# One of four weight sums per seven-product step: an adding transfer within SBUF in place of GpSimd

## The chip, the core and the metric

The kernel runs on one core of one Trainium2 chip, in one launch. Its time is device time in microseconds. The kernel before was timed three times: 1987.64, 1987.86 and 1988.36 us, with a median of 1987.86.

Five engines work from instruction queues of their own and meet only at semaphores: TensorE (PE in the profile; PEld is its weight load), VectorE (DVE), ScalarE (ACT), GpSimd (POOL) and SyncE (SP), which only issues transfers here.

## What is computed

The reference is one inference step of a two-layer encoder for 640 tokens (512 of a prompt, 8 streams of 16). Each layer is

```python
x = x + 0.5 * swiglu(rms_norm(x, norm_g[layer, 0]), w_gate, w_up, w_down)   # 1024 -> 2816 -> 1024
x = x + mixer(rms_norm(x, norm_g[layer, 1]))                                # attention and convolution, or pooling
x = x + 0.5 * swiglu(rms_norm(x, norm_g[layer, 2]), w_gate, w_up, w_down)

def swiglu(h, w_gate, w_up, w_down):
    return (jax.nn.silu(h @ w_gate) * (h @ w_up)) @ w_down
```

all in float32. The four feed-forward blocks (passes one to four in this text, `ffn0` to `ffn3` in the kernel) hold nearly all the work, and the change lies in them alone.

## The kernel before

**Products.** A float32 value is kept as a high part in TensorE's float32r form and a low part, the rest. Each product is three matmuls: high by high, high by low, low by high. ScalarE makes the high part by a copy that rounds (`fast_high`), DVE the low part by a subtraction (`fast_low`).

**Seven products for eight.** The hidden width of 2816 is 22 chunks of 128, in groups of 4, 6, 6 and 6 (`GROUPS`). Group 0 is done plainly. For the other three a step takes a 2 by 2 block of weights and a 2 by 2 block of inputs and forms seven block products instead of eight, in the manner of Strassen and Winograd; this needs sums of weight blocks. A pass has 26 such steps (`STEPS`, numbered 0 to 25): an *input step* handles one hidden chunk (gate and up: 7 products of 4 x 3 matmuls, weights 128x512 per block), an *output step* two output chunks of the down matrix (7 products of 3 x 3 matmuls, blocks of 128x384). Steps 0 to 5, 10 to 15 and 20 to 25 are input steps, 6 to 9 and 16 to 19 output steps.

**The weight sums.** The landed weights of a step are four blocks, `raw[0]` to `raw[3]`. GpSimd makes four sums in `block_and_weight_sums`, each as two instructions of half the columns (`weight_sum`, line 2401):

```python
weight_sum(raw[2], raw[2], raw[3], ALU.add, width)               # the block sum, in place
weight_sum(sums[:, 0], raw[2], raw[0], ALU.subtract, width)      # first sum
weight_sum(sums[:, 1], raw[3], sums[:, 0], ALU.subtract, width)  # second sum
weight_sum(sums[:, 2], raw[1], sums[:, 0], ALU.subtract, width)  # last sum
```

The first sum waits for part 3 of the step before to be split, because `sums` has one buffer; the last sum waits for part 4.

**Splits.** A step's weights go to TensorE in four parts: part 1 is `raw[0:2]`, part 2 is `raw[2:4]` after the block sum, part 3 the first and second sum, part 4 the last sum. In the time of step s ScalarE splits parts 3 and 4 of step s, then parts 1 and 2 of step s+1 (`in_step`), with the copies and activations that read finished products between; DVE follows the same order with the low parts.

**Loads.** SP loads the weights of step s+2 into the buffer of step s (two buffers, `in_raw`). The up half waits for part 2 of step s and for its second sum, the gate half also for its last sum (`in_free`). In each pass, after step 21's loads, SP waits for a product of step 19 and puts two loads of the down matrix (`out_raw`) in the queue ahead of step 22's weights.

**TensorE's order.** In step s TensorE runs the products of slots 0, 4, 1, 2, 6 of step s with those of slots 3 and 5 of step s-1 between (`product_order`). Slots 0 and 1 read part 1, slots 4 and 5 part 2, slots 2 and 3 part 3, slot 6 part 4. The first product of step s writes a bank that is free once DVE has made the low hidden product of step s-2 (`hidden_low`).

Of the kernel before, what the change touches and what calls it, by code (L numbers as in the profile page):

```python
# [9 lines left out]
ALU = mybir.AluOpType  # L10
# [71 lines left out]
N_STEPS = len(STEPS)  # L82
# [42 lines left out]
def product_at(s, slot):  # L125

    return len(PRODUCT_AT) * (s // N_STEPS) + PRODUCT_AT[s % N_STEPS, slot]
# [60 lines left out]
def landed(n):  # L188

    return 32 * (n // 2 + 1) + (32 if n >= IN_CHUNK["mix"] + 1 else 0)  # L190
# [17 lines left out]
def wait(eng, sem, value):  # L208

    if not isinstance(value, int) or value > 0:  # L210
        eng.wait_ge(sem, value)
# [35 lines left out]
def build(nc, ins, outs):  # L247
# [7 lines left out]
    with ExitStack() as stack:  # L255
# [131 lines left out]
        def sem(name):  # L387
            return keep(nc.semaphore(name))


        in_landed = [sem(f"in_landed{i}") for i in range(2)]
# [40 lines left out]

        sum_done, fast_hi, fast_split = sem("sum_done"), sem("fast_hi"), sem("fast_split")
        prod_mm, evac_done, gate_done = sem("prod_mm"), sem("evac_done"), sem("gate_done")
        block_made, block_hi, block_lo = sem("block_made"), sem("block_hi"), sem("block_lo")
# [74 lines left out]
        def in_free(eng, n, tile=0):  # L512

            old = n - 2
            if old < 0:
                return
            phase = [name for name, first in IN_CHUNK.items() if first <= old][-1]
            f = old - IN_CHUNK[phase]
            if phase in FFN_INDEX and f >= PLAIN:
                s = N_STEPS * FFN_INDEX[phase] + f - PLAIN  # L520
                eng.wait_ge(fast_split, 4 * s + 2)
                eng.wait_ge(sum_done, 4 * s + 4 - tile)
            else:
                eng.wait_ge(in_split, 2 * (SPLIT_CHUNK[phase] + f) + 2)

# [2 lines left out]
        def split_source(s, part):  # L528

            if part in (3, 4):  # L530
                return sums[:, 0:2, 0:width_of(s)] if part == 3 else sums[:, 2:3, 0:width_of(s)]
            return step_raw(s, load_number(s))[part - 1]

        def split_target(tensor, s, part):

            slots = tensor[:].rearrange("p j t (h k) c -> p (j t h) (k c)", h=2)
            chosen = {1: slice(0, 2), 2: slice(4, 8, 3) if s % N_STEPS % 2 else slice(4, 6), 3: slice(2, 4), 4: slice(6, 7)}[part]
            return slots[:, chosen, 0:width_of(s)]

        def step_raw(s, n):  # L540

            width = width_of(s)
            return [in_raw[:, n % 2, t, 0:2 * width // P].rearrange("p (h k) c -> p h (k c)", h=2) for t in range(2)]

        def width_of(s):

            return 4 * P if STEPS[s % N_STEPS][0] == "in" else 3 * P

        def load_number(s):

            return IN_CHUNK[FFN_PHASE[s // N_STEPS]] + PLAIN + s % N_STEPS
# [46 lines left out]
        def _(sp):  # L598
            def load_ffn_in(phase, layer, which, f):
                n = IN_CHUNK[phase] + f  # L600
                in_free(sp, n)
                for t, w in enumerate((w_gate, w_up)):
                    sp.dma_start(in_raw[:, n % 2, t],
                                 w[layer, which].rearrange("(k p) c -> p k c", p=P)[:, :, f * P:f * P + P]).then_inc(in_landed[n % 2], 16)
# [9 lines left out]
            def load_mix_in(c):  # L614
                n = IN_CHUNK["mix"] + c
                slot = n % 2
                in_free(sp, n)
                kind, j = MIX_CHUNKS[c]
                if kind == "q":

                    for g in range(2):
                        for t in range(2):
                            at = g * 256 + (2 * j + t) * 64
                            sp.dma_start(in_raw[:, slot, t, :, g * 64:g * 64 + 64], wi[:, :, at:at + 64]).then_inc(in_landed[slot], 16)
                    return
                at = {"kv": (512, 640), "conv": (1280 + 128 * j, 1792 + 128 * j), "gate": (768 + 256 * j, 896 + 256 * j)}[kind]
                for t in range(2):
                    sp.dma_start(in_raw[:, slot, t], wi[:, :, at[t]:at[t] + P]).then_inc(in_landed[slot], 16)
# [11 lines left out]
            def load_pool():  # L640
                n = IN_CHUNK["pool"]
                in_free(sp, n)
                for t in range(2):
                    src = pool_w[0, 2 * t:2 * t + 2].rearrange("g (k p) c -> p (g k) c", p=P)
                    dst = in_raw[:, n % 2, t].rearrange("p (q m) c -> p q (m c)", m=2)
                    sp.dma_start(dst, src).then_inc(in_landed[n % 2], 16)
# [584 lines left out]
        def _(act):  # L1231
# [63 lines left out]
            def fast_high(s, part):  # L1295


                n = load_number(s)
                act.wait_ge(in_landed[n % 2], landed(n))
                if s % N_STEPS:  # L1300
                    act.wait_ge(prod_mm, max(product_at(s - 1, slot) for slot in {1: (0, 1), 2: (4,), 3: (2, 3), 4: (6,)}[part]))
                if part == 2 and s % N_STEPS > 1:
                    act.wait_ge(prod_mm, product_at(s - 2, 5))
                if part > 1:
                    act.wait_ge(sum_done, 4 * s + {2: 1, 3: 3, 4: 4}[part])
                act.activation(split_target(in_hi, s, part), split_source(s, part), ACT.Copy).then_inc(fast_hi, 1)  # L1306

            def block_split(name):
                hi, _, made = block_parts[name]
                act.activation(hi[:], made[:], ACT.Copy).then_inc(block_hi, 1)  # L1310
# [331 lines left out]
            for step, (c, half) in enumerate(MIX_UNITS):  # L1642
# [21 lines left out]
                if step == 2:  # L1664
                    act.wait_ge(kv_turned, 1)
                    first, second = (psum[:, bank].rearrange("p (a b) -> p a b", a=4) for bank in (6, 7))
# [715 lines left out]
        def _(pool):  # L2382
            def less(index, made, a, b, newest):

                pool.wait_ge(block_made, 8 * index + MADE[newest])
                for k in range(4):
                    last = pool.tensor_tensor(made[:, k], a[:, k], b[:, k], ALU.subtract)
                last.then_inc(block_made, 1)
# [9 lines left out]
            def weight_sum(to, a, b, op, width):  # L2398

                for part in (slice(0, width // 2), slice(width // 2, width)):  # L2400
                    last = pool.tensor_tensor(to[:, part], a[:, part], b[:, part], op)  # L2401
                last.then_inc(sum_done, 1)

            def block_and_weight_sums(phase, index):

                if index == 3:
                    pool.wait_ge(rows_stored, 16 * 9)
                less(index, mix_f[1], b22_f, b12_f, "B22")
                less(index, b12_f, b12_f, b11_f, "T3")
                less(index, mix_f[0], b22_f, b12_f, "T1")  # L2410
                less(index, mix_f[2], b21_f, mix_f[0], "T2")
                for i in range(N_STEPS):
                    s = N_STEPS * index + i
                    n, width = load_number(s), width_of(s)
                    own = step_raw(s, n)
                    raw = [own[t][:, h] for t in range(2) for h in range(2)]
                    pool.wait_ge(in_landed[n % 2], landed(n))
                    weight_sum(raw[2], raw[2], raw[3], ALU.add, width)
                    if i == 0:
                        pool.wait_ge(block_lo, 7 * index + BLOCKS.index("B21") + 1)  # L2420
                    if s:
                        pool.wait_ge(fast_split, 4 * (s - 1) + 3)
                    pool.wait_ge(sum_done, 4 * s + 1)
                    weight_sum(sums[:, 0], raw[2], raw[0], ALU.subtract, width)
                    pool.wait_ge(sum_done, 4 * s + 2)
                    weight_sum(sums[:, 1], raw[3], sums[:, 0], ALU.subtract, width)
                    if s:
                        pool.wait_ge(fast_split, 4 * (s - 1) + 4)
                    weight_sum(sums[:, 2], raw[1], sums[:, 0], ALU.subtract, width)
# [19 lines left out]
            pool.wait_ge(line_stored, 16)  # L2449

            block_and_weight_sums("ffn0", 0)
            squares_sum(NORM["mix"], LAST_HALVES)
            pool.wait_ge(out_mm, OUT_UNIT["mix"])
# [20 lines left out]


            block_and_weight_sums("ffn1", 1)
            squares_sum(NORM["ffn2"], LAST_HALVES)
            block_and_weight_sums("ffn2", 2)
            pool.wait_ge(out_mm, OUT_UNIT["ffn2"] + 17)
            pool.wait_ge(conv_stored, 16 * 2)  # L2480
# [36 lines left out]
```

## Time and profile before

| | |
|---|---|
| median of three runs | 1987.86 us |
| the profiled execution | 1988.24 us |
| its span, first to last instruction | 1986.4 us |
| TensorE busy (matmuls) | 1978.6 us, 13462 matmuls |
| DVE / ACT / POOL busy | 1418.2 / 932.5 / 964.0 us |
| granted TensorE clock, mean | 0.999 of full speed |
| moved by DMA | 165.28 MB, mean 83 GB/s |

A timeline row merges neighbouring instructions of one line and form: start, length, engine, line, operation, output and inputs, shape, number of instructions; a bracket at its end is the idle time before it and what ended that. A matmul row is longer than the distance to the next, since matmuls are pipelined: the distance between starts is the pace.

### The profile page before, as it was taken

How to read it: one execution, taken by the hardware profiler on the slowest of the kernel's cores; microseconds unless marked ns; L12 is line 12 of the kernel's file. 1: busy time of each engine (PE TensorE's matmuls, PEld its weight loads, DVE VectorE, ACT ScalarE, POOL GpSimd, SP SyncE). 2: the span in 40 equal slices, each digit the busy share in tenths (PEclk: the TensorE clock that was granted, in tenths of full speed). 3: DMA queues.
4: the chain of work that ended last, by engine and by line, in shares of the span. 5: the costliest groups of instructions: out<-in, count | busy, mean ns of one | idle time of the engine just before them, and what ended most of it. 6: DMA issues, size and time to landing. Idle time of an engine off the chain costs nothing. (4 is left out here: it accounts for less than half of the span.)

```text
span 1986.4 us, 35197 instructions
## 1 busy us (share of the span) xinstructions
PE 1978.6 (100%) x13462; PEld 1957.5 (99%) x13462; DVE 1418.2 (71%) x2263; ACT 932.5 (47%) x1642; POOL 964.0 (49%) x1043
## 2 busy tenths in 40 slices
PE   9999999999999999999999999999999999999998
PEld 8999999999999999999999999999999999999998
DVE  5778687664766667878766668778767866878665
ACT  6354454543434435445455345454545535455443
POOL 2556666632000055676663336666743355666643
PEclk9999999999999999999999999999999999999999
DMA  6232324323222223232432222323332223232412
GB/s 162 74 86 70 101 70 117 101 58 95 66 64 65 56 73 86 77 95 69 117 102 75 64 65 75 96 80 91 102 109 70 67 57 86 77 99 65 122 38 86
DMA packets 312853, 165.28 MB, mean 83 GB/s; under 512 B 15539, under 2 KB 310271, under 8 KB 312688
## 3 DMA queue, kind: packets, MB, share of 16 engines
q1 hardware_dynamic: 307840, 157.31, 28.4%
q0 software_dynamic: 2672, 4.65, 1.0%
q8 instruction: 109, 1.79, 0.4%
q10 hardware_dynamic: 2176, 1.07, 0.2%
q14 instruction: 56, 0.46, 0.1%
HBM read 159.01 MB, written 4.00 MB: 82 GB/s over the span
## 5 line engine op out<-in xcount | busy, mean ns | idle before, releaser
L2401 POOL TENSOR_TENSOR sums<-in_raw,sums 128x256 f32<-128x256 f32 (+1 forms) x416 | 440.1, 1088 | 12.1 <-DVE in_lo L1751 3.9
L2401 POOL TENSOR_TENSOR sums<-in_raw 128x256 f32<-128x256 f32 (+1 forms) x208 | 179.9, 885 | 429.7 <-DVE in_lo L1751 377.4
L895 PE MATMUL psum<-xg_hi,in_lo 128*128 128x320 f32 x1152 | 356.0, 309 | 0.0
L893 PE MATMUL psum<-xg_hi,in_hi 128*128 128x320 f32 x1152 | 355.9, 309 | 0.0
L894 PE MATMUL psum<-xg_lo,in_hi 128*128 128x320 f32 x1152 | 355.9, 309 | 0.0
L1751 DVE TENSOR_TENSOR in_lo<-in_raw,in_hi 128x1024 fp32r<-128x1024 f32 (+1 forms) x208 | 271.9, 1309 | 42.5 <-ACT in_hi L1306 42.2
L893 PE MATMUL psum<-mix_hi,in_hi 128*128 128x320 f32 x864 | 267.0, 309 | 0.0
L894 PE MATMUL psum<-mix_lo,in_hi 128*128 128x320 f32 x864 | 267.0, 309 | 0.0
L895 PE MATMUL psum<-mix_hi,in_lo 128*128 128x320 f32 x864 | 267.0, 309 | 0.0
L1306 ACT ACTIVATE in_hi<-in_raw 128x1024 fp32r<-128x1024 f32 (+1 forms) x208 | 205.0, 991 | 111.7 <-PE psum L895 111.7
L744 PE MATMUL psum<-xg_hi,in_hi 128*128 128x320 f32 x800 | 252.3, 315 | 0.9 <-DVE in_lo L1792 0.6
L746 PE MATMUL psum<-xg_hi,in_lo 128*128 128x320 f32 x800 | 247.2, 309 | 0.0
L745 PE MATMUL psum<-xg_lo,in_hi 128*128 128x320 f32 x800 | 247.1, 309 | 0.0
L1306 ACT ACTIVATE in_hi<-sums 128x1024 fp32r<-128x1024 f32 (+1 forms) x208 | 156.6, 790 | 159.7 <-PE psum L895 124.2
L894 PEld LDWEIGHTS psum<-xg_lo,in_hi 128*128 128x128 f32 x1152 | 216.2, 188 | 0.0
L895 PEld LDWEIGHTS psum<-xg_hi,in_lo 128*128 128x128 f32 x1152 | 216.2, 188 | 0.0
L893 PEld LDWEIGHTS psum<-xg_hi,in_hi 128*128 128x128 f32 x1152 | 216.2, 188 | 0.0
L1751 DVE TENSOR_TENSOR in_lo<-sums,in_hi 128x1024 fp32r<-128x1024 f32 (+1 forms) x208 | 196.2, 967 | 18.1 <-ACT in_hi L1306 15.6
L744 PE MATMUL psum<-f_hi,f_out_hi 128*128 128x320 f32 x640 | 198.7, 311 | 0.3
L745 PE MATMUL psum<-f_lo,f_out_hi 128*128 128x320 f32 x640 | 197.8, 309 | 0.0
L746 PE MATMUL psum<-f_hi,f_out_lo 128*128 128x320 f32 x640 | 197.7, 309 | 0.0
L2401 POOL TENSOR_TENSOR in_raw<-in_raw 128x256 f32<-128x256 f32 (+1 forms) x208 | 168.9, 832 | 20.5 <-DMA in_raw<-in_ffn_w_gate 20.5
(267 smaller groups left out, 4560.9 us busy)
## 6 DMA issues: line engine op xcount, KB each, us to landing
in_raw<-in_ffn_w_gate SPq DMA_DIRECT2D x87, 512.0 KB, 5.2
in_raw<-in_ffn_w_up SPq DMA_DIRECT2D x86, 512.0 KB, 4.0
in_raw<-in_ffn_w_down SPq DMA_DIRECT2D x64, 384.0 KB, 4.0
out_raw<-in_ffn_w_down SPq DMA_DIRECT2D x32, 384.0 KB, 3.5
out_raw<-in_ffn_w_down SPq DMA_DIRECT2D x32, 256.0 KB, 2.9
in_raw<-in_mix_w_in SPq DMA_DIRECT2D x14, 512.0 KB, 4.6
out<-y_nat SPq DMA_DIRECT2D x5, 512.0 KB, 3.1
in_raw<-in_mix_w_in SPq DMA_DIRECT2D x8, 256.0 KB, 4.5
```

Source lines behind the costliest of these rows:

```text
L744: pe.matmul(dst, w_hi, v_hi, start=first, stop=False)
L745: pe.matmul(dst, w_hi, v_lo, start=False, stop=False)
L746: return pe.matmul(dst, w_lo, v_hi, start=False, stop=last)
L893: pe.matmul(dst, w_hi[:, k], v_hi, start=k == 0 and slot in (0, 1, 4), stop=False, skip_group_check=True)
L894: pe.matmul(dst, w_hi[:, k], v_lo, start=False, stop=False, skip_group_check=True)
L895: end = pe.matmul(dst, w_lo[:, k], v_hi, start=False, stop=k == wide - 1, skip_group_check=True)
L1306: act.activation(split_target(in_hi, s, part), split_source(s, part), ACT.Copy).then_inc(fast_hi, 1)
L1751: dve.tensor_tensor(split_target(in_lo, s, part), split_source(s, part), split_target(in_hi, s, part).bitcast(F32), ALU.subtract).then_inc ...
L2401: last = pool.tensor_tensor(to[:, part], a[:, part], b[:, part], op)
```

## The change

The block sum leaves GpSimd's arithmetic. In its place GpSimd issues a transfer whose source is `raw[3]` and whose destination is `raw[2]`, with the addition done by the transfer (`accum_op=ALU.add`). It reports on a semaphore of its own, `blocks_added`, which the first sum on GpSimd and part 2 on ScalarE now wait for. `sum_done` counts three sums per step instead of four. The transfer for step s+1 is issued between the second and the last sum of step s; the block sum for step s+1 stood behind the last sum of step s.

```diff
--- before.py
+++ after.py
@@ -432,6 +432,7 @@
 
 
 
+        blocks_added = sem("blocks_added")
         sum_done, fast_hi, fast_split = sem("sum_done"), sem("fast_hi"), sem("fast_split")
         prod_mm, evac_done, gate_done = sem("prod_mm"), sem("evac_done"), sem("gate_done")
         block_made, block_hi, block_lo = sem("block_made"), sem("block_hi"), sem("block_lo")
@@ -519,7 +520,7 @@
             if phase in FFN_INDEX and f >= PLAIN:
                 s = N_STEPS * FFN_INDEX[phase] + f - PLAIN
                 eng.wait_ge(fast_split, 4 * s + 2)
-                eng.wait_ge(sum_done, 4 * s + 4 - tile)
+                eng.wait_ge(sum_done, 3 * s + 3 - tile)
             else:
                 eng.wait_ge(in_split, 2 * (SPLIT_CHUNK[phase] + f) + 2)
 
@@ -1301,8 +1302,10 @@
                     act.wait_ge(prod_mm, max(product_at(s - 1, slot) for slot in {1: (0, 1), 2: (4,), 3: (2, 3), 4: (6,)}[part]))
                 if part == 2 and s % N_STEPS > 1:
                     act.wait_ge(prod_mm, product_at(s - 2, 5))
-                if part > 1:
-                    act.wait_ge(sum_done, 4 * s + {2: 1, 3: 3, 4: 4}[part])
+                if part == 2:
+                    act.wait_ge(blocks_added, 16 * (s + 1))
+                elif part > 2:
+                    act.wait_ge(sum_done, 3 * s + part - 1)
                 act.activation(split_target(in_hi, s, part), split_source(s, part), ACT.Copy).then_inc(fast_hi, 1)
 
             def block_split(name):
@@ -2401,6 +2404,13 @@
                     last = pool.tensor_tensor(to[:, part], a[:, part], b[:, part], op)
                 last.then_inc(sum_done, 1)
 
+            def add_in_place(s):
+
+                n = load_number(s)
+                second = step_raw(s, n)[1]
+                pool.wait_ge(in_landed[n % 2], landed(n))
+                pool.dma_start(second[:, 0], second[:, 1], accum_op=ALU.add).then_inc(blocks_added, 16)
+
             def block_and_weight_sums(phase, index):
 
                 if index == 3:
@@ -2409,21 +2419,23 @@
                 less(index, b12_f, b12_f, b11_f, "T3")
                 less(index, mix_f[0], b22_f, b12_f, "T1")
                 less(index, mix_f[2], b21_f, mix_f[0], "T2")
+                add_in_place(N_STEPS * index)
                 for i in range(N_STEPS):
                     s = N_STEPS * index + i
                     n, width = load_number(s), width_of(s)
                     own = step_raw(s, n)
                     raw = [own[t][:, h] for t in range(2) for h in range(2)]
-                    pool.wait_ge(in_landed[n % 2], landed(n))
-                    weight_sum(raw[2], raw[2], raw[3], ALU.add, width)
                     if i == 0:
                         pool.wait_ge(block_lo, 7 * index + BLOCKS.index("B21") + 1)
                     if s:
                         pool.wait_ge(fast_split, 4 * (s - 1) + 3)
-                    pool.wait_ge(sum_done, 4 * s + 1)
+                    pool.wait_ge(blocks_added, 16 * (s + 1))
+                    wait(pool, sum_done, 3 * s)
                     weight_sum(sums[:, 0], raw[2], raw[0], ALU.subtract, width)
-                    pool.wait_ge(sum_done, 4 * s + 2)
+                    pool.wait_ge(sum_done, 3 * s + 1)
                     weight_sum(sums[:, 1], raw[3], sums[:, 0], ALU.subtract, width)
+                    if i + 1 < N_STEPS:
+                        add_in_place(s + 1)
                     if s:
                         pool.wait_ge(fast_split, 4 * (s - 1) + 4)
                     weight_sum(sums[:, 2], raw[1], sums[:, 0], ALU.subtract, width)
```

On GpSimd, second pass, steps 21 and 22, the kernel before has these rows: the block sum of step 21 (its second half), its three sums, then the block sum of step 22 (the row that waits for `in_landed1`, the landed weights) and the first sum of step 22.

```order
L2401 TENSOR_TENSOR in_raw<-in_raw 128x256
L2401 TENSOR_TENSOR sums<-in_raw 128x256 [waits sum_done,fast_split]
L2401 TENSOR_TENSOR sums<-in_raw 128x256
L2401 TENSOR_TENSOR sums<-in_raw,sums 128x256 [waits sum_done]
L2401 TENSOR_TENSOR sums<-in_raw,sums 128x256
L2401 TENSOR_TENSOR sums<-in_raw,sums 128x256 [waits fast_split]
L2401 TENSOR_TENSOR sums<-in_raw,sums 128x256
L2401 TENSOR_TENSOR in_raw<-in_raw 128x256 [waits in_landed1]
L2401 TENSOR_TENSOR in_raw<-in_raw 128x256
L2401 TENSOR_TENSOR sums<-in_raw 128x256 [waits sum_done,fast_split]
```

The same place in the changed kernel, from the first sum of step 21 to the second sum of step 22:

```order
L2404 TENSOR_TENSOR sums<-in_raw 128x256 [waits sum_done,blocks_added,fast_split]
L2404 TENSOR_TENSOR sums<-in_raw 128x256
L2404 TENSOR_TENSOR sums<-in_raw,sums 128x256 [waits sum_done]
L2404 TENSOR_TENSOR sums<-in_raw,sums 128x256
L2412 DMA in_raw<-in_raw 128x512 [waits in_landed1]
L2404 TENSOR_TENSOR sums<-in_raw,sums 128x256 [waits fast_split]
L2404 TENSOR_TENSOR sums<-in_raw,sums 128x256
L2404 TENSOR_TENSOR sums<-in_raw 128x256 [waits sum_done,blocks_added,fast_split]
L2404 TENSOR_TENSOR sums<-in_raw 128x256
L2404 TENSOR_TENSOR sums<-in_raw,sums 128x256 [waits sum_done]
```

The wait for `in_landed1` has moved from behind the last sum of step 21 (the row that waits for `fast_split` alone) to ahead of it, and the row that carries it is an issue of a transfer.

On ScalarE, at the same step of the second pass, the kernel before has parts 3 and 4 of step 21, the split of a hidden block (`f_hi`), the copy of a product (`t`), part 1 of step 22, the activation of the low gate, part 2 of step 22:

```order
L1306 ACTIVATE in_hi<-sums 128x1024 [waits sum_done,prod_mm,in_landed0]
L1306 ACTIVATE in_hi<-sums 128x512 [waits sum_done,prod_mm,in_landed0]
L1379 ACTIVATE f_hi<-t2a 128x320 [waits hidden_done]
L1375 ACTIVATE t_51<-psum 128x320 [waits evac_done,prod_mm]
L1306 ACTIVATE in_hi<-in_raw 128x1024 [waits prod_mm,in_landed1]
L1364 ACTIVATE gate_low_74<-gate_low_74 128x320 [waits evac_done]
L1306 ACTIVATE in_hi<-in_raw 128x1024 [waits prod_mm,sum_done,in_landed1]
```

and the changed kernel:

```order
L1309 ACTIVATE in_hi<-sums 128x1024 [waits sum_done,prod_mm,in_landed0]
L1309 ACTIVATE in_hi<-sums 128x512 [waits sum_done,prod_mm,in_landed0]
L1382 ACTIVATE f_hi<-t2a 128x320 [waits hidden_done]
L1378 ACTIVATE t_51<-psum 128x320 [waits evac_done,prod_mm]
L1309 ACTIVATE in_hi<-in_raw 128x1024 [waits prod_mm,in_landed1]
L1367 ACTIVATE gate_low_74<-gate_low_74 128x320 [waits evac_done]
L1309 ACTIVATE in_hi<-in_raw 128x1024 [waits prod_mm,blocks_added,in_landed1]
```

Nothing moves on ScalarE; part 2 (the last row) waits for `blocks_added` where it waited for `sum_done`.

## Rows read from the trace of the kernel before

**Rows 1.** Busy time of each engine (us, x instructions), TensorE clock, DMA, by stretches.
```profile
705.00:995.00 290.00, 290.00 (x1976) 289.56 (x1975) 217.34 (x325) 136.06 (x223) 181.72 (x196) 1.00 0.30 82
...
1918.00:1986.00 68.00, 63.23 (x441) 62.46 (x439) 33.93 (x60) 22.67 (x42) 16.57 (x16) 0.99 0.18 63
```

**Rows 2.** Who TensorE waited for: us, times, longest; first and last of five.
```profile
PE psum L1026 <- DVE mean_r L2142: 1.1, 1, 1.1
...
PE psum L744 <- DVE x L1830: 0.2, 1, 0.2
```

**Rows 3.** TensorE timeline, 992 to 995: start, us, engine, line, operation.
```profile
992.71 0.31 PE L893 MATMUL psum<-xg_hi,in_hi 128*128 128x320 f32 x1
...
994.47 0.31 PE L893 MATMUL psum<-xg_hi,in_hi 128*128 128x320 f32 x1
```

**Rows 4.** GpSimd by groups: busy us, mean ns, idle before.
```profile
L2401 POOL TENSOR_TENSOR in_raw<-in_raw 128x256 f32<-128x256 f32 x144 | 118.1, 840 | 20.5 <-DMA in_raw<-in_ffn_w_gate 20.5
...
L2401 POOL TENSOR_TENSOR in_raw<-in_raw 128x192 f32<-128x192 f32 x64 | 50.9, 815 | 0.0
...
L2456 POOL DMA_DIRECT2D ck_nat<-in_cache_attn_k x1 | 1.0, 952 | 0.0
...
L2468 POOL DMA_DIRECT2D out<-kv_rows x1 | 0.6, 550 | 0.0
```

**Rows 5.** GpSimd timeline, 955 to 1005, second pass.
```profile
958.52 3.72 POOL L2401 TENSOR_TENSOR sums<-in_raw,sums 128x192 f32<-128x192 f32 x4
...
966.27 1.69 POOL L2401 TENSOR_TENSOR sums<-in_raw 128x256 f32<-128x256 f32 x2 [2.63 <-DVE in_lo L1751]
968.05 4.81 POOL L2401 TENSOR_TENSOR sums<-in_raw,sums 128x256 f32<-128x256 f32 x4
972.81 1.44 POOL L2401 TENSOR_TENSOR in_raw<-in_raw 128x256 f32<-128x256 f32 x2
...
978.34 4.81 POOL L2401 TENSOR_TENSOR sums<-in_raw,sums 128x256 f32<-128x256 f32 x4
988.59 1.80 POOL L2401 TENSOR_TENSOR in_raw<-in_raw 128x256 f32<-128x256 f32 x2 [5.44 <-DMA in_raw<-in_ffn_w_gate]
```

**Rows 6.** DMA issues, KB each, median us to landing; then all of `in_raw`.
```profile
cv_nat<-in_cache_attn_v POOLq DMA_DIRECT2D x1, 512.0 KB, 5.7
...
out<-kv_rows POOLq DMA_DIRECT2D x4, 64.0 KB, 2.2
...
DMA to landing us min/median/max: 3.1/4.4/9.6
```

**Rows 7.** ScalarE timeline, 955 to 1005.
```profile
974.04 1.58 ACT L1306 ACTIVATE in_hi<-sums 128x1024 fp32r<-128x1024 f32 x2 [0.93 <-PE psum L895]
...
985.92 1.58 ACT L1306 ACTIVATE in_hi<-sums 128x1024 fp32r<-128x1024 f32 x2 [1.37 <-PE psum L895]
...
987.76 0.42 ACT L1375 ACTIVATE t<-psum 128x320 f32<-128x320 f32 x1
989.45 1.07 ACT L1306 ACTIVATE in_hi<-in_raw 128x1024 fp32r<-128x1024 f32 x1 [1.27 <-PE psum L895]
```

**Rows 8.** Who GpSimd waited for: us, times, longest.
```profile
POOL in_raw L2401 <- DMA in_raw<-in_ffn_w_gate: 20.5, 4, 5.4
```

**Rows 9.** GpSimd timeline, 335 to 355, first pass.
```profile
343.29 2.00 POOL L2401 TENSOR_TENSOR in_raw<-in_raw 128x256 f32<-128x256 f32 x2 [4.86 <-DMA in_raw<-in_ffn_w_gate]
```

**Rows 10.** DVE timeline, 955 to 1005.
```profile
988.75 1.03 DVE L1921 TENSOR_TENSOR f_lo<-t2a,f_hi 128x320 fp32r<-128x320 f32 x1
...
990.54 1.81 DVE L1751 TENSOR_TENSOR in_lo<-in_raw,in_hi 128x1024 fp32r<-128x1024 f32 x1 [0.36 <-ACT in_hi L1306]
992.28 0.49 DVE L1896 TENSOR_TENSOR psum<-psum,gate_low 128x320 f32<-128x320 f32 x1
992.68 1.36 DVE L1751 TENSOR_TENSOR in_lo<-in_raw,in_hi 128x1024 fp32r<-128x1024 f32 x1
993.96 0.48 DVE L1921 TENSOR_TENSOR f_lo<-psum,f_hi 128x320 fp32r<-128x320 f32 x1
```

## The prediction

> **What bounds the kernel now.** I read four views in this order: the busy time of each engine by stretches, TensorE's list of waits, GpSimd's list of waits, and the timelines of single engines around one step. The first answers nearly the whole question. In the middle stretch of the second feed-forward pass TensorE is busy 290.00 us of 290.00; in the last 68 us of the program it is busy 63.23 [rows 1]. Its waits come to five entries, of which the longest is 1.1 us and the shortest 0.2 us, and none stands on the seven-product lines 893 to 895 [rows 2]. TensorE starts a matmul every (994.47 - 992.71) / 12 = 0.147 us without a hole [rows 3], and at that pace an input step (84 matmuls) lasts 12.3 us and an output step (63) 9.2 us. So the time is TensorE's work, and nothing that GpSimd does today is waited for where the change acts. The change can win almost nothing; the question is only whether it makes TensorE wait.
>
> **What goes.** The change takes 208 GpSimd instructions away: 144 of 840 ns and 64 of 815 ns, 118.1 + 50.9 = 169 us of GpSimd time [rows 4]. Worth on the path: nothing, since GpSimd idles in every step. The gain is bounded by what TensorE idles in these stretches, 0.00 us.
>
> Beside DVE instructions that read two operands from SBUF the same GpSimd sum takes far longer: a pair runs 1.44 us at one place and, as half of 4.81, 2.4 us at another [rows 5]. The Trainium skill's page "SBUF — State Buffer" (SBUF: two separate sides) says that a GpSimd operation that reads SBUF and such a DVE operation exclude each other for the whole instruction; by it the change also shortens DVE's low parts, and if DVE were waited for, up to those 169 us would count. The trace agrees on the lengthening, but TensorE's waits for DVE come to 1.1 us at most and none lies on the seven-product lines [rows 2]. That rule's gain is rival 3 below.
>
> **What comes.** 104 accumulating transfers issued by GpSimd. Issuing costs GpSimd 0.55 us for 128 rows (the `kv_rows` store), and 0.95 us for a transfer of many short pieces (`ck_nat`) [rows 4]. This one has 128 rows of 2 or 1.5 KB, like `kv_rows`; I take 0.55 and keep 0.95 as the far end. How long it takes to land no row shows, since no transfer before adds. The nearest rows are the GpSimd-issued transfers of 64 KB at 2.2 us and of 512 KB at 5.7 us; the longest landing of any load into `in_raw` is 9.6 us [rows 6]. Here 256 KB (192 KB in output steps) are read, added to what is read at the destination, and written; I take 4 us, nearer the middle of 2.2 and 5.7, and keep 2.2 and 9.6 as ends.
>
> The Trainium skill's page "Collectives: The Full Stack" (The bandwidth ceiling) says that an adding transfer pays for two source reads, not for the addition. By that it moves like 512 KB, an estimate of 5.7 us from the same row instead of 4; no run here shows it yet. The next paragraph shows that the sum is the same with either.
>
> **What covers it.** The transfer for step s+1 is issued when GpSimd has finished the second sum of step s, and what it makes is wanted when GpSimd takes up the first sum of step s+1. Around the end of the output steps the second sum of step 19 ends at 958.52 + 3.72 / 2 = 960.4 and the first of step 20 starts at 966.27: 5.9 us [rows 5]. So 4 us, 5.7 us too, cost nothing: the GpSimd idle time (waiting for DVE) hides them. Past that there is more cover: the two sums of step 20 end at 968.05 + 2.4 = 970.5, and ScalarE takes them up at 974.04 [rows 5, 7], 3.5 us later. A single landing of 9.4 us would do no harm. ScalarE's split of the added block itself comes later than GpSimd's first sum. The second new cost, 0.55 us on GpSimd ahead of the last sum of every step, falls into the same idle time, and so does the 0.55 us by which the next gate load (which waits for the last sum) leaves later.
>
> **The one place without cover.** The transfer's wait for the landed weights now stands ahead of the last sum of the step before; until now it stood behind it. Four times in the program, 20.5 us in all, GpSimd waits there [rows 8]: at step 22 of each pass, whose weights are queued behind two loads of the down matrix. In the second pass the wait lasts 5.44 us and ends at 988.59; in the first 4.86, that is 0.6 us less late against TensorE's pace [rows 5, 9]; passes three and four repeat the two values (the four make the 20.5). Before, the last sum of step 21 had been done since 978.34 + 4.81 = 983.15. Now it is queued behind this wait, and behind it ScalarE's fourth part of step 21, DVE's, and everything that follows them in their order:
> - GpSimd: wait ends 988.6, issue 0.55, last sum 1.44 (a pair with DVE idle, as DVE then is): 990.6.
> - ScalarE: fourth part 0.6 (the pair of 1.58 less 1.07 for a part of the third's size, a little rounded up), to 991.2; then the hidden split and the copy, 0.7 from the end of that pair to the end of the copy [rows 7]: 991.9. TensorE's last product of step 21 needs this copy and DVE's fourth low part (about 991.9) and starts at 992.71 [rows 3]: it still holds, by 0.8 us. Then the first part of step 22, 1.07: 993.0.
> - DVE: low fourth part until 991.9; then hidden low and gate, 990.54 - 988.75 less the 0.36 of idle time = 1.43 [rows 10]: 993.3; low first part of step 22, 1.74 to the next start: 995.05; the hidden product, 0.49: 995.5.
> - TensorE's first product of step 22 needs both of these and starts at 994.47 today [rows 3]. It is late by 1.05 us.
>
> If DVE runs alone (its hidden low 0.48 rather than 1.03, its low part 1.36 rather than 1.81 [rows 10]), 1.0 us goes and nothing is late. So passes two and four lose 0 to 1.1 us each, passes one and three 0 to 0.5: together 0 to 3.2 us, and I take the middle, 1.6. With the far ends (issue 0.95, the last sum contended at 2.4) each pass loses 1.4 more: 8.8 us. A lost microsecond of TensorE isn't made up later, as it has no idle time to give back.
>
> **The sum.** The profiled execution took 1988.24 us, a span of 1986.4 and 1.84 around it, and lies 0.38 above the median of the three runs, 1987.86. 1988.24 - 0 + 1.6 = 1989.8 in its terms, 1989.5 against the median. Less than 0.2% (4 us) is no change that a measurement of this kernel can tell.
>
> **Rivals.**
> 1. The wait at step 22 weighs more: slower. Mechanism as above, with the far ends of the two prices: 8.8 us, 1996.7; it counts as slower once the four passes lose more than 4 us, that is one microsecond each. For it: every link stands in order behind the landed weights. Against it: DVE is idle when that sum runs, and the issue resembles the 0.55 us row. Chance 0.18.
> 2. The adding transfer is slow everywhere: slower. At 9.6 us the loop of an output step (two sums, 3.7 us, and the transfer) takes 13.3 us against TensorE's 9.2, 4.1 us lost per step. The first landing of four is late by 9.6 - 5.9 - 3.5 = 0.2 us, the fourth by 0.2 + 3 x 4.1 = 12.5; there are eight such groups of four: 100 us, 2088. It begins to decide at 9.2 - 3.7 = 5.5 us kept up over several steps. For it: no row shows an addition, and the loads share the transfer engines. Against it: 5.7 us is the landing of twice the bytes. Chance 0.06.
> 3. Faster, as GpSimd and DVE are relieved. This needs TensorE idle time, of which the passes have none. Even all 68.00 - 63.23 = 4.77 us of its idle time in the last stretch [rows 1], which the change doesn't touch, would only just reach 0.2%: 1983.1. Chance 0.02.
>
> My forecast, no change within 0.2% with 0 to 3.2 us lost, has 0.74. The slower cases make 0.18 + 0.06, and 0.24 is what I give to slower by over 0.2%; faster 0.02. The range goes from 1987.0 (nothing lost, and the spread of the runs below the median) to 1996.0, which takes in nearly all of rival 1 and leaves out rival 2 and the far end.
>
> **What will show it.** Right: GpSimd loses its sums on `in_raw` (about 170 us busy less), gains 104 issues of about 0.55 us, and the adding transfers land within 2.2 to 5.9 us; GpSimd's wait for the gate weights at step 22 is now ahead of the last sum of step 21, four times; TensorE's waits on the seven-product lines come to at most about 3 us, all at the first product of step 22. Wrong: landing above 6 us, GpSimd or ScalarE waiting for the added block in most steps, or TensorE idle in the output steps; or a wait at step 22 well above 1 us a pass.

## The result, and the profile after

The changed kernel takes 2020.03 us (median of four runs, 2019.15 to 2021.21) against 1988.11 of the kernel before (four runs, 1987.64 to 1988.83): a ratio of 1.016, 95% interval 1.0147 to 1.0173. It is 32 us slower, where 1989.5 was forecast in a range that ended at 1996.0. The profiled span grew from 1986.4 to 2017.5 us, 31.1 more.

Read in the order of the forecast, the first view already tells that the passes have holes: the same stretch as in [rows 1], and the last 68 us of the program.

```profile
705.00:995.00 290.00, 284.33 (x1932) 283.00 (x1931) 217.99 (x320) 131.70 (x215) 145.01 (x168) 1.00 0.40 95
...
1949.00:2017.00 68.00, 63.31 (x442) 62.54 (x440) 33.93 (x60) 22.68 (x42) 16.57 (x16) 0.99 0.18 63
```

TensorE is busy 284.33 of 290 us, where it was busy for all of them; the end of the program is as it was. Who TensorE waited for (us in all, times, longest), beside [rows 2]:

```profile
PE psum L894 <- DVE pair_low L1899: 20.8, 16, 1.3
PE psum L894 <- DVE psum L1899: 1.9, 3, 0.9
PE psum L894 <- DVE x L1942: 1.9, 2, 1.0
PE psum L745 <- DVE f_out_lo L1749: 1.9, 4, 0.5
```

Five new entries, all for DVE, none for GpSimd or for a transfer; the fifth, of 0.2 us, is left out here. The first is the finding: 16 waits for `pair_low`, the low hidden product of the odd input steps, four in each pass (at steps 3, 5, 13 and 15). The next views show one of them, at step 3 of the second pass. TensorE first, beside [rows 3]:

```profile
792.16 0.31 PE L896 MATMUL psum<-xg_hi,in_lo 128*128 128x320 f32 x1
793.76 0.41 PE L894 MATMUL psum<-xg_hi,in_hi 128*128 128x320 f32 x1 [1.29 <-DVE pair_low L1899]
```

From start to start that is 1.60 us in place of 0.147. Counted this way the 16 holes cost 23.4 us, four at the start of the first output stage 2.5, three at step 22 of passes two to four 2.4, and two on the fold of `x` 2.2: 30.5 of the 31.1. (The list of waits has less, since it takes the modelled end of the matmul before.) DVE at that place:

```profile
789.66 0.87 DVE L1920 TENSOR_TENSOR ht_lo<-psum,ht_hi 128x320 fp32r<-128x320 f32 x2
790.45 2.85 DVE L1754 TENSOR_TENSOR in_lo<-in_raw,in_hi 128x1024 fp32r<-128x1024 f32 x1
793.23 0.48 DVE L1899 TENSOR_TENSOR pair_low<-psum,gate_low 128x320 f32<-128x320 f32 x1
```

and the same place before, 7.65 us earlier:

```profile
782.00 0.87 DVE L1917 TENSOR_TENSOR ht_lo<-psum,ht_hi 128x320 fp32r<-128x320 f32 x2
782.80 1.26 DVE L1751 TENSOR_TENSOR in_lo<-in_raw,in_hi 128x1024 fp32r<-128x1024 f32 x1
783.98 0.48 DVE L1896 TENSOR_TENSOR pair_low<-psum,gate_low 128x320 f32<-128x320 f32 x1
```

DVE comes to its split of part 1 at the same time, but takes 2.85 us over it instead of 1.26, so `pair_low` is ready at 793.71 instead of 784.46 + 7.65 = 792.11. Before, TensorE started on it at

```profile
784.65 0.31 PE L893 MATMUL psum<-xg_hi,in_hi 128*128 128x320 f32 x1
```

so 784.65 - 784.46 = 0.19 us of slack was all there was (0.17 to 0.19 at the 16 places), and of that TensorE needs 0.05 to start (793.71 to 793.76 after the change). That leaves 1.60 - 0.14 = 1.46 us of hole. GpSimd at the same place, after the change:

```profile
786.15 1.69 POOL L2404 TENSOR_TENSOR sums<-in_raw 128x256 f32<-128x256 f32 x2 [5.59 <-DVE in_lo L1754]
787.91 2.02 POOL L2404 TENSOR_TENSOR sums<-in_raw,sums 128x256 f32<-128x256 f32 x2
789.88 0.86 POOL L2412 DMA_DIRECT2D in_raw<-in_raw  x1
790.49 1.72 POOL L2404 TENSOR_TENSOR sums<-in_raw,sums 128x256 f32<-128x256 f32 x2
```

and before (the second row holds the second and the last sum, the third the block sum of the next step):

```profile
778.50 1.69 POOL L2401 TENSOR_TENSOR sums<-in_raw 128x256 f32<-128x256 f32 x2 [4.22 <-DVE in_lo L1751]
780.26 4.40 POOL L2401 TENSOR_TENSOR sums<-in_raw,sums 128x256 f32<-128x256 f32 x4
784.62 2.67 POOL L2401 TENSOR_TENSOR in_raw<-in_raw 128x256 f32<-128x256 f32 x2
```

The issue at 789.88 pushes the last sum back by 0.6 us, so that both of its halves now fall into DVE's split. They are hardly stretched (1.72 us for both, against [rows 5]'s 1.44 alone), and DVE's instruction ends 793.30 - 792.21 = 1.09 us after them: it has waited both out. Before, it was DVE that went through, between the two halves of the last sum, and GpSimd that was stretched.

Two of the smaller groups of holes come of the same meeting. At the start of the first output stage the last sum meets DVE's `mix_lo` (four places), and in the first output step of passes one and four its `f_lo` (two places); what DVE does next, `f_out_lo` and the fold of `x`, comes late by it. After the change, and then before:

```profile
747.11 3.17 DVE L1760 TENSOR_TENSOR mix_lo<-mix_f,mix_hi 128x1280 fp32r<-128x1280 f32 x1
299.76 2.20 DVE L1924 TENSOR_TENSOR f_lo<-pair_odd,f_hi 128x320 fp32r<-128x320 f32 x1
```

```profile
740.13 2.03 DVE L1757 TENSOR_TENSOR mix_lo<-mix_f,mix_hi 128x1280 fp32r<-128x1280 f32 x1
294.07 0.88 DVE L1921 TENSOR_TENSOR f_lo<-pair_odd,f_hi 128x320 fp32r<-128x320 f32 x1
```

So 23.4 + 2.5 + 2.2 = 28.1 us are DVE waiting for the last sum, and 2.4 are step 22.

The transfer itself is as forecast. Its issue and its landing (KB, median us), beside [rows 4, 6]:

```profile
L2412 POOL DMA_DIRECT2D in_raw<-in_raw x104 | 90.1, 866 | 41.3 <-DMA in_raw<-in_ffn_w_gate 31.7 <-DMA in_raw<-in_ffn_w_down 8.3 <-issue 1.2
```

```profile
in_raw<-in_raw POOLq DMA_DIRECT2D x72, 256.0 KB, 3.7
...
in_raw<-in_raw POOLq DMA_DIRECT2D x32, 192.0 KB, 3.0
```

The record of the issue is 0.87 us long, but the next instruction starts 0.61 us after it (789.88 to 790.49). Of the 31.7 us of idle time ahead of it for gate weights 30.0 are the four waits of [rows 8], which have moved with it; they come to more than 20.5 as GpSimd now reaches them earlier, with the last sum still to do.

### The profile page after: what moved, and what is told of

Its sections match the earlier page's. It is cut to its first block and busy times, and to the rows that moved or that the text cites. A ratio compares the mean times of both kernels' runs of the same rounds, so it can differ in the third digit from the quotient of the medians.

```text
span 2017.5 us, 35096 instructions
## 1 busy us (share of the span) xinstructions
PE 1982.6 (98%) x13462; PEld 1956.9 (97%) x13462; DVE 1431.6 (71%) x2263; ACT 932.5 (46%) x1642; POOL 818.8 (41%) x939
## 5 line engine op out<-in xcount | busy, mean ns | idle before, releaser
L2404 POOL TENSOR_TENSOR sums<-in_raw 128x256 f32<-128x256 f32 (+1 forms) x208 | 173.8, 856 | 589.8 <-DVE in_lo L1754 508.9
L2404 POOL TENSOR_TENSOR sums<-in_raw,sums 128x256 f32<-128x256 f32 (+1 forms) x416 | 405.9, 1034 | 8.2
L1754 DVE TENSOR_TENSOR in_lo<-in_raw,in_hi 128x1024 fp32r<-128x1024 f32 (+1 forms) x208 | 293.5, 1412 | 42.9 <-ACT in_hi L1309 42.4
L894 PEld LDWEIGHTS psum<-xg_hi,in_hi 128*128 128x128 f32 x1152 | 216.2, 188 | 28.1 <-DVE pair_low L1899 25.0
L894 PEld LDWEIGHTS psum<-mix_hi,in_hi 128*128 128x128 f32 x864 | 162.2, 188 | 0.0
```

Source lines behind the costliest of these rows:

```text
L894: pe.matmul(dst, w_hi[:, k], v_hi, start=k == 0 and slot in (0, 1, 4), stop=False, skip_group_check=True)
L1754: dve.tensor_tensor(split_target(in_lo, s, part), split_source(s, part), split_target(in_hi, s, part).bitcast(F32), ALU.subtract).then_inc ...
```

## The experiments

Each run is the changed kernel or the kernel before with one edit. All times are medians beside runs of the kernel before at 1987.8 to 1988.0. The diffs leave out the lines that set up the scratch columns `marks` and the semaphore `marked`.

**The transfer behind the last sum.**

```diff
-                    if i + 1 < N_STEPS:
-                        add_in_place(s + 1)
                     if s:
                         pool.wait_ge(fast_split, 4 * (s - 1) + 4)
                     weight_sum(sums[:, 2], raw[1], sums[:, 0], ALU.subtract, width)
+                    if i + 1 < N_STEPS:
+                        add_in_place(s + 1)
```

> The changed kernel, with the adding transfer issued behind the last sum of a step where it stood ahead of it; the same 104 transfers. Theory (GpSimd's issue pushes the last sum by 0.6 us into DVE's low split of part 1, which then waits both halves out: 1.26 us becomes 2.85, at 16 places): 1988 to 1990 us, all of those splits back near 1.26 us, no wait of TensorE on pair_low. Rival A (the traffic of the adding transfers slows DVE or the loads): stays at 2015 to 2020. Rival B (the wait for the landed weights ahead of the last sum at step 22 is the loss): falls too, but then only by the 2 us that TensorE's holes there show, to 2018.

Measured: 1994.00 us (1992.55 to 1996.59), ratio 1.0029 [1.0018, 1.0041]. The waits on `pair_low` are gone, those at step 22 and at the start of the output stage too, and 26 of the 32 us with them. But 6 remain, and the expectation of 1988 to 1990 missed them. The list of TensorE's waits has a single new entry, for the fold of `x` at the last output step of a group:

```profile
PE psum L894 <- DVE x L1942: 6.0, 6, 1.5
```

At the longest, the transfer left at 853.41 and the gate load, which the same last sum sets free, at 853.54. GpSimd and ScalarE then wait for the added block:

```profile
853.41 0.85 POOL L2412 DMA_DIRECT2D in_raw<-in_raw  x1
861.06 1.43 POOL L2404 TENSOR_TENSOR sums<-in_raw 128x256 f32<-128x256 f32 x2 [6.80 <-DMA in_raw<-in_raw]
```

```profile
861.02 1.06 ACT L1309 ACTIVATE in_hi<-in_raw 128x1024 fp32r<-128x1024 f32 x1 [3.07 <-DMA in_raw<-in_raw]
```

The landing took about 7.5 us there, and its median for 256 KB is 5.7 where it was 3.7:

```profile
in_raw<-in_ffn_w_gate SPq DMA_DIRECT2D x87, 512.0 KB, 6.5
in_raw<-in_raw POOLq DMA_DIRECT2D x72, 256.0 KB, 5.7
```

So in this place the transfer's traffic (rival A) seems to cost something, by another way: it meets a load of 512 KB, which itself takes 6.5 us where it took 5.2 in the kernel before. The last experiment puts this to the test.

**Only the issue, without the addition**: the kernel before with a transfer of 4 bytes a row between scratch columns at the place in question.

```diff
+                    if i + 1 < N_STEPS:
+                        m = 1 * (s - index)
+                        wait(pool, marked, 16 * m)
+                        for k in range(1):
+                            pool.dma_start(marks[:, 2 * k:2 * k + 1], ident[:, 0:1]).then_inc(marked, 16)
                     if s:
                         pool.wait_ge(fast_split, 4 * (s - 1) + 4)
                     weight_sum(sums[:, 2], raw[1], sums[:, 0], ALU.subtract, width)
```

> The kernel before, all four sums on GpSimd, plus one transfer of 128 rows of 4 bytes between two scratch columns, issued ahead of the last sum of each step at the place where the changed kernel issues its adding transfer; it waits for no weights. Theory: the 0.6 us of issue alone does the damage, 16 x 1.47 = 23.5 us more: 2011 (2006 to 2018), with DVE's part 1 at 2.9 us at those places. Rival A (traffic of the adding transfers): 1988 to 1990. Rival B (landed wait): 1988 to 1990.

Measured: 2042.19 us (2032.32 to 2042.57), ratio 1.0259 [1.0239, 1.0278]: the sign is as the theory says, and no adding transfer and no wait for weights is needed for it; the size is more than twice the expected. Here the block sum still follows the last sum, and DVE waits for four halves at step 3 and 13:

```profile
794.50 0.55 POOL L2433 DMA_DIRECT2D marks<-ident  x1
795.07 1.45 POOL L2403 TENSOR_TENSOR sums<-in_raw,sums 128x256 f32<-128x256 f32 x2
796.46 1.41 POOL L2403 TENSOR_TENSOR in_raw<-in_raw 128x256 f32<-128x256 f32 x2
```

```profile
795.07 3.90 DVE L1753 TENSOR_TENSOR in_lo<-in_raw,in_hi 128x1024 fp32r<-128x1024 f32 x1
```

In the profiled execution (span 2030.3, 43.9 more than before) the 16 holes cost 29.6 us from start to start, and four at the start of the output stage 6.5. Another 4.7 go to a lower granted clock behind three of the eight long holes, 0.57 in this stretch, mostly the 1.2 GHz level of the two:

```profile
258.00:262.00 4.00, 3.66 (x14) 3.66 (x15) 2.23 (x4) 1.30 (x4) 0.00 (x0) 0.57 0.30 90
```

The hole just ahead of it was 2.6 us from start to start; behind the five others of that size the clock stayed full. That leaves 3.1 us of the 43.9 unplaced. The profiled execution is the shortest of the four (2032.32); the three near 2042 show a lower mean clock, 0.993 to 0.995 against 0.997, and their further 10 us are not placed, as there is no trace of them.

**Only four steps.** The transfer goes behind the last sum at 16 of 104 places:

```diff
+                    behind = i in (3, 5, 13, 15)
-                    if i + 1 < N_STEPS:
+                    if i + 1 < N_STEPS and not behind:
                         add_in_place(s + 1)
...
+                    if i + 1 < N_STEPS and behind:
+                        add_in_place(s + 1)
```

> The changed kernel, with the adding transfer behind the last sum at steps 3, 5, 13 and 15 of each pass alone (16 of 104), ahead of it elsewhere. Theory: 2020.0 - 16 x 1.47 = 1996.5 (1994 to 1999), what is left being the holes at step 22 and on the fold of x. Rival A: 2020. Rival B: 2020.

Measured: 1995.69 us (1993.38 to 2000.40), ratio 1.0035 [1.0023, 1.0047]. As expected: these 16 places hold 24 of the 32 us.

**A short last sum at the same four steps**, with the issue ahead of it. The kernel leaves out the other 496 columns of that sum:

```diff
-                    weight_sum(sums[:, 2], raw[1], sums[:, 0], ALU.subtract, width)
+                    weight_sum(sums[:, 2], raw[1], sums[:, 0], ALU.subtract, 16 if i in (3, 5, 13, 15) else width)
```

> The changed kernel, but at steps 3, 5, 13 and 15 of each pass the last sum takes 16 columns of 512 (the rest of it is left out); the transfer is issued ahead of it as in the changed kernel. Theory (the last sum on GpSimd and DVE's split shut each other out): there is next to nothing to wait out, DVE's part 1 takes 1.2 to 1.5 us: 1996.5 (1994 to 1999). Rival C (it is not the sum that holds DVE, but the issue, or the traffic of the transfer that lands just then): 2015 to 2020.

Measured: 1995.1 us (1993.88 to 2001.46), ratio 1.004 [1.0026, 1.0055]. The issue, the transfer and its landing are where they were in the changed kernel, and DVE's part 1 beside them takes

```profile
783.69 1.21 DVE L1754 TENSOR_TENSOR in_lo<-in_raw,in_hi 128x1024 fp32r<-128x1024 f32 x1
```

So neither the issue nor the traffic holds DVE by itself, and rival C falls: it takes the full sum behind the issue. Here the short sum was the one to wait. Its two halves of 8 columns come to 1.40 us, of which the first takes 1.23 and ends 0.06 us after DVE:

```profile
783.73 1.40 POOL L2404 TENSOR_TENSOR sums<-in_raw,sums 128x8 f32<-128x8 f32 x2
```

**A longer delay.** A second, small issue between the adding transfer and the last sum:

```diff
                         add_in_place(s + 1)
+                        wait(pool, marked, 16 * (s - index))
+                        pool.dma_start(marks[:, 0:1], ident[:, 0:1]).then_inc(marked, 16)
```

> The changed kernel with a second issue (128 rows of 4 bytes between scratch columns) between the adding transfer and the last sum, so that the last sum starts another 0.6 us later. Theory (whichever of GpSimd's last sum and DVE's part 1 starts first shuts the other out; in the changed kernel GpSimd is first by 0.04 us, 790.49 against 790.53): DVE is now first, its part 1 takes about 1.3 us at the 16 places, TensorE no longer waits on pair_low, and the longer delay makes the kernel faster: 1996.5 plus up to 4 us for step 22 and the start of the output stage, 1994 to 2003. Rival C (what costs is that the last sum and all behind it come late): slower than 2020, 16 x 0.6 more: 2030.

Measured: 1996.15 us (1995.41 to 1996.27), ratio 1.0038 [1.0024, 1.0052]. The last sum starts 0.6 us later still, and the kernel is 24 us faster than the changed one:

```profile
782.75 0.85 POOL L2442 DMA_DIRECT2D marks<-ident  x1
783.33 3.14 POOL L2406 TENSOR_TENSOR sums<-in_raw,sums 128x256 f32<-128x256 f32 x2
```

```profile
782.75 1.44 DVE L1756 TENSOR_TENSOR in_lo<-in_raw,in_hi 128x1024 fp32r<-128x1024 f32 x1
784.11 0.47 DVE L1901 TENSOR_TENSOR pair_low<-psum,gate_low 128x320 f32<-128x320 f32 x1
```

DVE goes through and GpSimd is stretched (3.14 us for two halves), as in the kernel before. At these 16 places a late last sum costs nothing; one that meets DVE at the wrong moment does. What is left stands mostly around the start of step 22, whose wait now holds two issues: holes of 5.5 us from start to start in passes two to four.

**The small issue behind the last sum**, in the kernel before:

```diff
                     weight_sum(sums[:, 2], raw[1], sums[:, 0], ALU.subtract, width)
+                    if i + 1 < N_STEPS:
+                        wait(pool, marked, 16 * (s - index))
+                        pool.dma_start(marks[:, 0:1], ident[:, 0:1]).then_inc(marked, 16)
```

> The kernel before with the small transfer of 128 rows of 4 bytes issued behind the last sum, where it was ahead of it in the run at 2042. Theory (the place of the issue matters, not the issue): 1987 to 1990, no wait on pair_low. Rival C' (104 issues cost by themselves, through queues or GpSimd time): most of the 54 us stays.

Measured: 2001.71 us (2001.05 to 2002.96), ratio 1.0068 [1.0054, 1.0081]. The waits on `pair_low` are gone, but 13.7 us stay, neither theory's number. The issue now pushes the block sum of the next step, and that meets other DVE instructions with two operands in SBUF: a split of the down matrix at the start of the output stage (four holes, 4.6 us),

```profile
746.34 2.42 DVE L1748 TENSOR_TENSOR f_out_lo<-out_raw,f_out_hi 128x512 fp32r<-128x512 f32 x1
```

and a product sum in the first output step (eight places, about 6 us),

```profile
833.71 1.37 DVE L1914 TENSOR_TENSOR psum<-pair_odd,pair_even 128x320 f32<-128x320 f32 x1
```

which took 1.14 and 0.49 us before. Same mechanism, another victim. At the first of these places DVE starts 0.43 us ahead of the block sum, during the issue, and still ends 0.56 us after it:

```profile
746.17 0.58 POOL L2434 DMA_DIRECT2D marks<-ident  x1
746.77 1.43 POOL L2403 TENSOR_TENSOR in_raw<-in_raw 128x256 f32<-128x256 f32 x2
```

The remaining 3 us are not placed.

**The transfer behind the last sum, and the gate load behind the transfer.** `in_free` is what SyncE waits for before a load; the edit of the first experiment comes with it and is not shown again:

```diff
                 eng.wait_ge(sum_done, 3 * s + 3 - tile)
+                if tile == 0 and (s + 1) % N_STEPS:
+                    eng.wait_ge(blocks_added, 16 * (s + 2))
```

> The adding transfer behind the last sum (as in the run at 1994.0), and the gate load that the same last sum frees waits until the adding transfer has landed. Theory on what was left there (adding transfer and 512 KB load leave at the same moment, the 256 KB then land in 5.7 us instead of 3.7, and the fold of x on DVE comes late behind ScalarE's part 2, 6.0 us of TensorE's waits): landing back to 4 us or less, no waits on the fold: 1988 to 1990. Rival E (the loads have no slack for 4 us of delay): GpSimd or ScalarE wait for gate weights in most steps, 1994 or more. If the landing isn't shortened, the load wasn't what lengthened it, and the time stays at 1994.

Measured: 1987.58 us (1986.82 to 1989.31, 11 runs) against 1987.97, ratio 0.9998 [0.9989, 1.0007]. The landing is short again, the gate load shorter than in the kernel before (3.9 us against 5.2, where it left about 1 us behind the up load and now leaves later), and TensorE's list of waits is back to entries of 1.1 us and less:

```profile
in_raw<-in_ffn_w_gate SPq DMA_DIRECT2D x87, 512.0 KB, 3.9
in_raw<-in_raw POOLq DMA_DIRECT2D x72, 256.0 KB, 3.7
```

```profile
PE psum L1029 <- DVE mean_r L2147: 1.1, 1, 1.1
```

So the 32 us are undone with the adding transfers kept. It doesn't beat the kernel before: GpSimd is busy 870.8 us instead of 964.0 and DVE 1399.7 instead of 1418.2, and neither was waited for.

## Why the prediction was wrong

The step that failed is one sentence of "What covers it": "The second new cost, 0.55 us on GpSimd ahead of the last sum of every step, falls into the same idle time". The price was right (0.61 us), and the idle time was there; the issue did not make GpSimd late for anyone. It put two instructions into the time, and ahead, of another engine's instruction that excludes them. Covering a delay with idle time is not enough where the two engines shut each other out.

The means to see it stood in the prediction. It read the exclusion off GpSimd's rows (1.44 against 2.4 us) [rows 5] and used it as a possible gain alone, with the argument that TensorE's waits name DVE for 1.1 us at most [rows 2]. No wait only says that slack is not negative. It was 0.17 to 0.19 us at these 16 places, and of the loss of 1.6 us on DVE 1.46 went into TensorE: 23.4 us of the 31.1. A term "last sum against DVE's part 1, 1.44 us less 0.19, at 16 to 104 places" would have given 20 us and more as the far end.

That the issue ahead of the full last sum is what costs is shown from both sides: the issue does it without any adding transfer, and with the issue behind the sum, or a short sum behind the issue, the waits on `pair_low` are gone. How the issue does it is not shown. The reading above is the shift of 0.6 us. The rival is that a sum straight behind an issue doesn't give way to DVE as one behind another sum does. In the kernel before, and in the runs at 1994.0 and 1987.58, no DVE instruction with two operands in SBUF takes over 1.0 us more than the shortest of its kind; in the changed kernel 22 do, and these, like those of the other five runs, all stand beside a sum whose first half follows straight upon an issue. A delay of 0.6 us without an issue would tell the two apart, and no run has one.

The Trainium skill's page "SBUF — State Buffer" (Who interferes with whom) states that a DVE instruction with two inputs in SBUF contends with a GpSimd instruction that reads SBUF, and that issue order decides who blocks. By that rule moving the last sum could turn a loss on GpSimd into one on DVE. The traces agree on the exclusion, 1.26 us becoming 2.85 and 3.90. On the order they agree only in part (below).

The other points:
- What goes is worth nothing on the path: right. The run at 1987.58 has the whole relief and gains 0.02%, within the interval. Rival 3 is out.
- 104 transfers that land within 2.2 to 5.9 us: right, 3.7 and 3.0 us. Rival 2 is out. By the two-reads rule of the Trainium skill's page "Collectives: The Full Stack" (The bandwidth ceiling), which the page gives for the adding steps of a ReduceScatter, the estimate was 5.7 us; the 3.7 measured here lies below that.
- The place without cover, step 22, 0 to 3.2 us with 1.6 taken: right in place and size. Holes of 2.4 us at the first product of step 22 in passes two to four, and none in the run with the transfer behind the last sum.
- Rival 1, step 22 as the way to slower: the right side with the wrong mechanism, and 8.8 us at its far end where 32 came.
- None of the marks of being wrong came: GpSimd waits for the added block at 10 of 104 places, and the first product of step 22 loses 1.1 us a pass at most. What failed is a mark of being right, "at most about 3 us, all at the first product of step 22": TensorE's waits on the seven-product lines come to 24.6 us, 22.7 of them at other steps.

## What to carry to other kernels

Before an instruction is put ahead of another on GpSimd, look at what DVE does in the time into which that other one moves; if both read SBUF and DVE reads two operands there, price it as that overlap, for whichever engine loses. Where the bound engine shows no wait, work out the slack of each of its suppliers before calling a delay covered. And a transfer that is freed by the same event as a large load should leave well ahead of it, or hold the load back: here that was worth 6 us. A lead of 0.13 us was not enough (5.7 us to landing); in the changed kernel, at 3.7 us, the lead was 2.5 us in the median.

## What was not expected of the hardware

- More delay can cost less: with the last sum 0.6 us later the kernel loses 32 us, with 1.2 us 8.
- DVE, once it waits, can be passed by several sums of GpSimd: two in the changed kernel and four in the run with the small issue (3.90 us). What decides who goes first is open. Start order as the trace has it does not: DVE starts 0.04 us ahead of the sum in the changed kernel (790.45 and 790.49) and waits 1.6 us; with the short sum it starts 0.04 us ahead too (783.69 and 783.73) and waits for nothing. With the small issue behind the last sum it starts 0.43 us ahead (746.34 and 746.77) and waits 1.7 us; with two issues 0.58 us ahead (782.75 and 783.33), and goes through. Counting DVE from the end of its instruction before (790.53), as the expectation of the two-issue run does, doesn't help: the short sum was ahead by that count too (783.73 against 783.76).
- The addition within SBUF of 256 KB lands in 3.7 us in the changed kernel, where the gate load leaves 2.5 us behind it in the median, and in 5.7 where that load of 512 KB leaves 0.13 us behind it. That load takes 6.5 then, 5.2 in the kernel before, and 3.9 when it is held back. The Trainium skill's page "DMA: Bandwidth & Descriptors" (Issuing engines are not separate DMA queues) says that transfers of all engines share the same transfer engines, and these numbers agree.
